# State reads of the sample group with 32 query columns as weights, updates by 32 rows, and waits for the tile that is needed

## The chip, the cores and the metric

The kernel runs on one NeuronCore of a Trainium2 chip. It is one launch, and the time is what the device takes for it, in microseconds. The figure quoted is the median of repeated runs. A profile is taken of one further execution, and its durations are those of that execution alone.

The engines that matter here are the tensor engine (PE; its weight loads are listed apart as PEld), the vector engine (DVE), the scalar engine (ACT), GpSimd (POOL) and the sync engine (SP), which issues all DMAs. Each works off its own list of instructions in order and waits on semaphores for the others.

## The reference

Two layers of a decoder trunk are applied to 320 tokens: one prompt of 256, and 8 sample sequences of 8 tokens each. In each layer three mixers of 4 heads carry a state of 128x128 per sequence and head (A: mLSTM, B: retention, C: a gated linear recurrence). For mixer B, in short:

```python
s = jnp.einsum('bthd,bshd->bhts', qc, kc) * dec
o = jnp.einsum('bhts,bshv->bthv', s, vc) + jnp.einsum('bthk,bhkv->bthv', qc, S) * inter
S_new = chunk_dec * S + jnp.einsum('hs,bshk,bshv->bhkv', to_end, kc, vc)
```

So each head reads its state (`qc` times `S`) and updates it (`k` times `v`, weighted). A and C do the same with other weights, and A also divides by a normaliser. A fourth branch (D) is a short convolution. Each layer then has gates, projections, two layer norms and a feed-forward part of width 4096. All weights and data are float32.

## The kernel before, in words

Activations stand with features on the 128 partitions and the 320 tokens along the free dimension (`T`, columns 256 to 319 are the samples). The big products go through 181 weight slots a layer (`SLOTS`). A slot is one 128x1024 block of weights. It is brought by DMA into a ring of three, split into a high part (`whi`, by ACT or DVE) and a low part (`wlo`, by POOL), and used in three products of 320 columns for each of its 8 blocks (lines 1179 to 1181) into one of three banks `gps`. A finished output is a tile; ACT or DVE takes it out of its bank and counts that in `tile_free`.

The mixers run as stages between the slots. `schedule_of_layer` writes the order once: a stage stands behind a slot when its inputs are there and some slots have passed since the last one (`COST`). Each stage is a list of phases by engine (`PHASES`), and each phase names the phases for which it waits; every finished phase is counted in `mix_done`. The banks `xp0` to `xp4` belong to the stages.

Two stages of each of the 24 heads (12 a layer) are changed:

- `num` reads. PE transposes the keys into `xp0` (`turn`, line 1290), adds up scores times values in `xp3` (`weigh`, lines 1301 to 1303), and adds the state reads (line 1364): for each of the 8 sequences a matmul that loads the 128x128 state `s0` as weights and streams 8 columns of `qw`, the weighted queries. ACT then copies the keys to `kt` (line 660) and the result on. DVE makes `vm` (line 1006), the sample values once per sequence, masked, 64x1024.
- `fin` updates. PE forms the prompt's new state (line 1375) and the samples' 8 updates (line 1383), two matmuls with 64 rows and 512 columns. DVE adds them into `s0` (line 1027), and SP sends it out and loads the state of the head after the next into the same buffer.

In mixer A a stage `a_score` and in B `b_rope` and `b_score` (line 1295 is the scores' first matmul, line 984 the last operation of `b_rope` on DVE) go ahead of `num`; `a_sq` (A) and `b_mean` (B) come between `num` and `fin`. In A `vm` is made in `a_sq`.

An f32 matmul is one instruction and shows as two records in the trace. Its form, as 128*128, is the part of the array it uses: rows times columns.

Beside the phases' own waits stands `settled`. Ahead of every stage's matmuls, and of a stage whose first phase is on ACT or DVE, the engine waits until all tiles up to the previous slot have left their banks:

```python
n = layer * NTILE + tile - tiles_in(i) - crossed(i)
for e in ("act", "dve"):
    if freed(e, n):
        eng.wait_ge(tile_free[e], freed(e, n))
```

Line numbers here and in the rows are those of this kernel; the changed one has its own, in the rows on the change.

## Time and profile before

| | |
|---|---|
| median of 3 runs | 1700.25 us (1698.64 to 1701.16) |
| the profiled execution | 1694.1 us, of which the span from first to last instruction is 1692.3 |
| PE busy | 1599.3 us, 95% of the span |
| PEld busy | 1520.7 us, 90% |
| DVE busy | 925.0 us, 55% |
| ACT busy | 648.0 us, 38% |
| POOL busy | 899.0 us, 53% |
| granted clock of PE, mean | 0.965 of full speed |
| L1364, state reads | 384 records |
| L1383, updates | 96 records |

A matmul's duration in the profile includes the time it spends in the pipeline, so durations of consecutive ones overlap. What a stretch costs on PE is read from the distance between starts. A line of the timeline merges equal neighbours: its first number is the first start, the second the time from there to the last end, and x is the count. The idle time ahead of a line, with what released it, stands in brackets.

### The profile page before, as it was taken

The numbers are of one execution on the slowest core, as the hardware profiler recorded it, in microseconds if no ns is written. First come the engines' busy times: TensorE is split into PE (matmuls) and PEld (weight loads), VectorE is DVE, ScalarE is ACT, GpSimd is POOL, SyncE is SP. The second block draws the span as 40 slices with busy tenths as digits, with TensorE's granted clock in tenths as the row PEclk, the third lists the DMA queues.
The fourth block names the chain that finished last, engine by engine and source line by source line (L and its number), as shares of the span: only waits on it lengthen the run. The fifth ranks groups of instructions, "written<-read, shape, count | busy, mean of one in ns | idle before, by whom it ended". The sixth has DMA issues, their size and how long they took to land.

```text
span 1692.3 us, 25612 instructions
## 1 busy us (share of the span) xinstructions
PE 1599.3 (95%) x10258; PEld 1520.7 (90%) x10258; DVE 925.0 (55%) x1717; ACT 648.0 (38%) x1166; POOL 899.0 (53%) x390
## 2 busy tenths in 40 slices
PE   7899999999999879999898999999999998799997
PEld 7899989998899869999797998889989997799996
DVE  4864774246766864422547657643457669544124
ACT  5434343333434343333354344333334343334333
POOL 6455453434445556666755554433444555566664
PEclk9999998999999989999999999989989999899998
DMA  7333443333444424444433334433334443344442
GB/s 271 111 116 108 165 155 113 114 114 127 129 160 142 125 87 150 150 150 150 128 121 110 104 115 163 141 116 111 114 115 153 127 138 115 97 150 150 150 150 82
DMA packets 66254, 223.57 MB, mean 132 GB/s; under 512 B 8024, under 2 KB 12632, under 8 KB 66136
## 3 DMA queue, kind: packets, MB, share of 16 engines
q1 hardware_dynamic: 66136, 221.93, 41.3%
q8 instruction: 82, 1.34, 0.3%
q14 instruction: 36, 0.29, 0.1%
HBM read 206.33 MB, written 15.58 MB: 131 GB/s over the span
## 4 chain that ended last, share of the span: by engine, by line
PE 80%; DVE 14%; ACT 2%; issue 2%; DMA 0%; SPq 0%; DVEq 0%; ACTq 0%
PE gps L1179 22%; PE gps L1180 21%; PE gps L1181 21%; PE xp L1383 3%; PE xp L1364 3%; DVE mix L918 1%; PE xp L1324 1%; PE xp L1384 1%; PE xp L1301 1%; DVE rs L1074 1%; PE xp L1303 1%; DVE whi L778 1%; PE xp L1375 1%; DVE mix L806 1%; DVE mix L1109 1%
## 5 line engine op out<-in xcount | busy, mean ns | idle before, releaser
L550 POOL TENSOR_TENSOR wlo<-raw,whi 128x1024 fp32r<-128x1024 f32 x362 | 878.0, 2427 | 765.4 <-ACT whi L571 463.3
L1179 PE MATMUL gps<-xh,whi 128*128 128x320 f32 x2000 | 649.7, 325 | 43.9 <-DVE xl L1119 22.4
L1180 PE MATMUL gps<-xl,whi 128*128 128x320 f32 x2000 | 631.5, 316 | 0.0
L1181 PE MATMUL gps<-xh,wlo 128*128 128x320 f32 x2000 | 631.1, 316 | 0.0
L571 ACT ACTIVATE whi<-raw 128x1024 fp32r<-128x1024 f32 x258 | 273.3, 1059 | 516.0 <-PE gps L1181 456.2
L1179 PEld LDWEIGHTS gps<-xh,whi 128*128 128x128 f32 x2000 | 389.0, 194 | 52.9 <-issue 31.7
L1180 PEld LDWEIGHTS gps<-xl,whi 128*128 128x128 f32 x2000 | 388.9, 194 | 3.2 <-issue 0.4
L1181 PEld LDWEIGHTS gps<-xh,wlo 128*128 128x128 f32 x2000 | 387.8, 194 | 0.0
L1179 PE MATMUL gps<-ah,whi 128*128 128x320 f32 x640 | 200.5, 313 | 0.5
L1180 PE MATMUL gps<-al,whi 128*128 128x320 f32 x640 | 199.1, 311 | 0.0
L1181 PE MATMUL gps<-ah,wlo 128*128 128x320 f32 x640 | 199.1, 311 | 0.0
L1179 PEld LDWEIGHTS gps<-ah,whi 128*128 128x128 f32 x640 | 121.3, 190 | 1.8 <-DVE al L841 0.8
L778 DVE CAST whi<-raw 128x1024 fp32r<-128x1024 f32 x104 | 76.4, 734 | 84.5 <-PE gps L1181 57.3
L1180 PEld LDWEIGHTS gps<-al,whi 128*128 128x128 f32 x640 | 121.4, 190 | 0.3
L1181 PEld LDWEIGHTS gps<-ah,wlo 128*128 128x128 f32 x640 | 121.4, 190 | 0.0
L824 DVE TENSOR_TENSOR mix<-mix,gps 128x320 f32<-128x320 f32 x32 | 15.6, 488 | 162.4 <-PE gps L1181 162.0
L819 DVE TENSOR_TENSOR gps<-gps,tt 128x320 f32<-128x320 f32 x64 | 32.0, 500 | 123.7 <-ACT tt L590 123.7
L597 ACT ACTIVATE tt<-gps,prm 128x320 f32<-128x320 f32 x64 | 33.8, 529 | 139.6 <-PE gps L1181 139.6
L1179 PE MATMUL gps<-yh,whi 128*128 128x320 f32 x256 | 80.9, 316 | 3.4 <-DVE al L841 2.1
L1180 PE MATMUL gps<-yl,whi 128*128 128x320 f32 x256 | 79.0, 309 | 0.0
L1181 PE MATMUL gps<-yh,wlo 128*128 128x320 f32 x256 | 79.0, 309 | 0.0
L1019 DVE COPY pst<-xp 128x128 f32<-128x128 f32 x24 | 7.0, 292 | 90.0 <-PE xp L1384 90.0
(271 smaller groups left out, 1925.2 us busy)
## 6 DMA issues: line engine op xcount, KB each, us to landing
raw<-in_w SPq DMA_DIRECT2D x362, 512.0 KB, 3.5
s<-in_st SPq DMA_DIRECT2D x24, 512.0 KB, 4.5
out_ss<-s SPq DMA_DIRECT2D x24, 512.0 KB, 2.7
con<-in_cst SPq DMA_DIRECT2D x4, 526.0 KB, 5.4
out_sp<-pst SPq DMA_DIRECT2D x24, 64.0 KB, 2.6
mix<-in_x SPq DMA_DIRECT2D x4, 320.0 KB, 5.0
out_y<-mix SPq DMA_DIRECT2D x8, 160.0 KB, 1.9
ee<-in_cst SPq DMA_DIRECT2D x1, 224.0 KB, 3.8
```

The source lines that it names most:

```text
L550: nc.gpsimd.tensor_tensor(wlo[:, c % RING, :, :], raw[:, c % RING, :, :], whi[:, c % RING, :, :].bitcast(F32), ALU.subtract).then_inc(lo_d ...
L571: nc.scalar.activation(whi[:, c % RING, :, :], raw[:, c % RING, :, :], ACT.Copy).then_inc(hi_done["act"], 1)
L597: link(nc.scalar.activation(t, ps, ACT.Abs, bias=prm[:, layer, PBG + j:PBG + j + 1]))
L778: V.tensor_copy(whi[:, c % RING, :, :], raw[:, c % RING, :, :]).then_inc(hi_done["dve"], 1)
L806: link(V.tensor_tensor(mix[:, a, :], xh[:, a, :].bitcast(F32), xl[:, a, :].bitcast(F32), ALU.add))
L819: link(V.tensor_tensor(ps, ps, t, ALU.mult))
L918: done(V.tensor_tensor(z, b, b[:, :, 0:1].to_broadcast([P, T // 4, 4]), ALU.subtract))
L1179: M(out, hi, xhi, start=start, stop=False)
L1180: M(out, hi, xlo, start=False, stop=False)
L1181: return M(out, lo, xhi, start=False, stop=stop)
L1364: last = M(xp[3][:, SEQ + b * DS:SEQ + (b + 1) * DS], s0[:, j % 2, b, :], qw[:, h, s], start=False, stop=b == NB - 1, skip_group_check=True)
L1383: M(xp[1 + i][:, :], kt[0:NS, 2, :], vm[:, 4 * i:4 * i + 4, :], start=True, stop=True)
```

## The change

The state reads swap sides. The weights are now 32 columns of `qw`, from the first query of a sequence on, and the state streams past them as 128 moving columns. The result is 32x128; only its first 8 rows belong to the sequence, the others are not used. Four such matmuls go to the four column strips of the array (`tile_position` (0, 32 i)) and to the four groups of 32 partitions of `xp4`, two rounds for 8 sequences. `qw` is 24 columns wider for it, zeroed once. ACT copies the 128x256 result to `seen`, and two matmuls with `seen` as weights and 32 chosen columns of the identity add it, turned, to `xp3`. The reads stand ahead of the transposes now.

The updates use row strips. `vm` holds 4 sequences side by side instead of 8 (64x512): the upper 32 rows belong to sequences 0 to 3, the lower to 4 to 7. Four matmuls of 32 rows and 256 columns replace two of 64 and 512, and alternate between the row strips and between banks `xp1` and `xp2`. The masks are folded to 4 columns (`same`, `fade` once, `own` once a head of A).

`settled` waits for the last tile that the stage uses (`last_tile_of`), and only in the stage's first phase. `num` has five phases instead of three, in C and B for instance:

```diff
-    "numC": (("pe", ("fin", -1, 1)), ("act", (0, ("fin", -1, 3))), ("dve", 0)),
-    "numA": (("pe", (("a_score", 0, 3), ("fin", -1, 2))), ("act", 0), ("dve", 1)),
-    "a_sq": (("act", ("num", 0, 2)), ("dve", ("num", 0, 0))),
-    "numB": (("pe", (("b_score", 0, 1), ("fin", -1, 2))), ("act", (0, ("fin", -1, 3))), ("dve", 0)),
-    "b_mean": (("pe", ("num", 0, 1)), ("dve", 0), ("act", 1)),
-
-    "finC": (("pe", (("num", 0, 1), ("num", 0, 2))), ("dve", 0), ("act", (0, ("fin", -1, 3))), ("dve", 2)),
...
+    "numC": (("pe", ("fin", -1, 2)), ("act", 0), ("pe", ("fin", -1, 1)), ("act", (2, ("fin", -1, 3))), ("dve", 2)),
...
+def last_tile_of(stage, n, h):
+
+    if n == "D":
+        return LTILES.index(("in", "bD", h) if stage == "conv" else ("br", "A", KD - 1))
+    name = {"c_log": ("in", "fC", 2 * h + 1), "c_first": ("in", "qC", h), "a_gate": ("in", "ifA", 0),
+            "a_score": ("in", "kA", h), "b_rope": ("in", "kB", h), "num": ("vt", "v" + n, h),
+            "fin": ("in", {"C": "gC", "A": "oA", "B": "gB"}[n], h)}.get(stage)
+    return None if name is None else LTILES.index(name)
...
-        def settled(eng, layer, tile, i):
-
-
-            n = layer * NTILE + tile - tiles_in(i) - crossed(i)
+        def settled(eng, layer, stage, n, h):
+
+
+            last = last_tile_of(stage, n, h)
+            if last is None:
+                return
+            n = layer * NTILE + last + 1
...
                elif stage == "num" and k == 1:
+                    done(nc.scalar.activation(seen[:, :, :], xp[4][:, 0:2 * P].rearrange("p (r c) -> p r c", r=2), ACT.Copy))
+                elif stage == "num":
...
-                        ends, mask = (ee[:, 255:256], ee[:, 383:384]), ee[0:NS, 384 + DS - 1:SP4:DS]
+                        ends, mask = (ee[:, 255:256], ee[:, 383:384]), own[:, :]
+                        half = 384 + NQ * DS
+                        link(V.tensor_tensor(own[:, :], ee[0:NS, 384 + DS - 1:half:DS], ee[0:NS, half + DS - 1:SP4:DS],
+                                             ALU.add))
...
-                    done(V.tensor_tensor(vm[:, :, :], v_of(n, h, 2).unsqueeze(1).to_broadcast([NS, NB, P]),
-                                         mask.unsqueeze(2).to_broadcast([NS, NB, P]), ALU.mult))
+                    done(V.tensor_tensor(vm[:, :, :], v_of(n, h, 2).unsqueeze(1).to_broadcast([NS, NQ, P]),
+                                         mask.unsqueeze(2).to_broadcast([NS, NQ, P]), ALU.mult))
...
+            def read_states(j, h):
+
+                for r in range(2):
+                    for i in range(4):
+                        b = 4 * r + i
+                        q = qw[:, h, b * DS:b * DS + 32]
+                        last = M(xp[4][32 * i:32 * (i + 1), r * P:(r + 1) * P], q, s0[:, j % 2, b, :], start=True, stop=True,
+                                 tile_position=(0, 32 * i), skip_group_check=True)
+                return last
+
+            def add_states
...
+                pick = ident.rearrange("p (i t) -> p i t", t=32)[:, :, 0:DS]
+                for r in range(2):
+                    out = xp[3][:, SEQ + 32 * r:SEQ + 32 * (r + 1)].rearrange("p (i t) -> p i t", t=DS)
+                    last = M(out, seen[:, r, :], pick, start=False, stop=r == 1, skip_group_check=True)
+                return last
...
+                elif stage == "num" and k == 0:
+                    j = layer * HEADS_PER_LAYER + state_of(n, h)
+                    pe.wait_ge(s_in[j % 2], 16 * (j // 2 + 1))
+                    done(read_states(j, h))
                 elif stage == "num":
-                    j = layer * HEADS_PER_LAYER + state_of(n, h)
                     turn(xp[0], z12[:, 1, h, :] if n == "C" else k_of(n, h))
-                    pe.wait_ge(s_in[j % 2], 16 * (j // 2 + 1))
                     weigh(xp[3], lambda i: v_of(n, h, i), h)
-                    for b in range(NB):
-                        s = slice(b * DS, (b + 1) * DS)
-                        last = M(xp[3][:, SEQ + b * DS:SEQ + (b + 1) * DS], s0[:, j % 2, b, :], qw[:, h, s],
-                                 start=False, stop=b == NB - 1, skip_group_check=True)
+
+                    follow(pe, layer, [("act", rows[1][2])])
+                    last = add_states()
...
-                    for i in range(2):
-                        M(xp[1 + i][:, :], kt[0:NS, 2, :], vm[:, 4 * i:4 * i + 4, :], start=True, stop=True)
+                    for j in range(0, NQ, 2):
+                        for i in range(2):
+
+                            rows = slice(32 * i, 32 * (i + 1))
+                            M(xp[1 + i][:, j * P:(j + 2) * P], kt[rows, 2, :], vm[rows, j:j + 2, :], start=True,
+                              stop=True, tile_position=(32 * i, 0), skip_group_check=True)
...
-                        settled(pe, layer, tile, slot_i)
-                        phase(*item[1:], layer, lambda ins: ins.then_inc(mix_done["pe"], 1))
+                        if k == 0:
+                            settled(pe, layer, *item[1:])
+                        phase(*item[1:], k, layer, rows, lambda ins: ins.then_inc(mix_done["pe"], 1))
```

On PE, the second head of mixer C in the first layer, before: stage `num`. The names after the arrow are the operands, `con` is the constants, among them the identity, `mix` the keys of C, `pt` the scores.

```order
L1290 MATMUL xp<-con,mix 128x128 [waits tile_free_dve,tile_free_act,mix_done_dve]
L1290 MATMUL xp<-con,mix 128x128
L1290 MATMUL xp<-con,mix 64x128
L1301 MATMUL xp<-pt,vc 128x256 [waits s_in0]
L1302 MATMUL xp<-pt,vc 128x128
L1303 MATMUL xp<-pt,vc 128x64
L1364 MATMUL xp<-qw,s 128x8 x8
```

Stage `fin` of the same head, a weight slot later, with the slot's product ahead and behind:

```order
L1181 MATMUL gps<-xh,wlo 128x320
L1375 MATMUL xp<-vc,kt 128x128 [waits tile_free_act,tile_free_dve,mix_done_dve,mix_done_act]
L1375 MATMUL xp<-vc,kt 128x128
L1383 MATMUL xp<-vm,kt 128x512 x2
L1384 MATMUL xp<-sq,ones 128x320
L1179 MATMUL gps<-xh,whi 128x320 [waits tile_free_act,lo_done]
```

`num` now:

```order
L1339 MATMUL xp<-s,qw 32x128 [waits s_in0,tile_free_act,mix_done_act]
L1339 MATMUL xp<-s,qw 32x128 x7
L1318 MATMUL xp<-con,mix 128x128 [waits mix_done_dve]
L1318 MATMUL xp<-con,mix 128x128
L1318 MATMUL xp<-con,mix 64x128
L1329 MATMUL xp<-pt,vc 128x256
L1330 MATMUL xp<-pt,vc 128x128
L1331 MATMUL xp<-pt,vc 128x64
L1348 MATMUL xp<-con,seen 128x32 [waits mix_done_act]
L1348 MATMUL xp<-con,seen 128x32
```

And `fin` now:

```order
L1209 MATMUL gps<-xh,wlo 128x320
L1422 MATMUL xp<-vc,kt 128x128 [waits tile_free_act,tile_free_dve,mix_done_dve,mix_done_act]
L1422 MATMUL xp<-vc,kt 128x128
L1433 MATMUL xp<-vm,kt 128x256 x4
L1435 MATMUL xp<-sq,ones 128x320
L1207 MATMUL gps<-xh,whi 128x320 [waits tile_free_act,lo_done]
```

The reads have moved from behind the weighing to the head of the stage, the load of the state (`s_in0`) is waited for there, and two matmuls with a wait on ACT end it. The updates are four instead of two.

On PE, `b_score` of B's first head, before and now:

```order
L1181 MATMUL gps<-yh,wlo 128x320
L1295 MATMUL xp<-zc 128x256 [waits tile_free_dve,tile_free_act,mix_done_dve]
L1296 MATMUL xp<-zc 128x128
L1297 MATMUL xp<-zc 64x64
L1179 MATMUL gps<-yh,whi 128x320 [waits tile_free_dve,lo_done]
```

```order
L1209 MATMUL gps<-yh,wlo 128x320
L1323 MATMUL xp<-zc 128x256 [waits mix_done_dve]
L1324 MATMUL xp<-zc 128x128
L1325 MATMUL xp<-zc 64x64
L1207 MATMUL gps<-yh,whi 128x320 [waits tile_free_dve,lo_done]
```

The matmuls are the same; the waits on `tile_free` are gone.

On DVE, the last of a gate tile and stage `a_sq` of A's first head, before and now:

```order
L828 TENSOR_SCALAR gps<-gps,prm 128x320 [waits act_part]
L829 TENSOR_TENSOR tt<-gps,tt 128x320 [waits dve_chain]
L1005 TENSOR_SCALAR vw<-va,ee 128x128 [waits mix_done_pe]
L1005 TENSOR_SCALAR vw<-va,ee 128x128
L1006 TENSOR_TENSOR vm<-va,ee 64x1024
L832 TENSOR_TENSOR mix<-gps,zc 128x320 [waits slot_done,gate_ready,tile_free_dve] x2
```

```order
L850 TENSOR_SCALAR gps<-gps,prm 128x320 [waits act_part]
L851 TENSOR_TENSOR tt<-gps,tt 128x320 [waits dve_chain]
L1021 TENSOR_TENSOR own<-ee 64x4 [waits mix_done_pe]
L1030 TENSOR_SCALAR vw<-va,ee 128x128 [waits dve_chain]
L1030 TENSOR_SCALAR vw<-va,ee 128x128
L1031 TENSOR_TENSOR vm<-va,own 64x512
L854 TENSOR_TENSOR mix<-gps,zc 128x320 [waits slot_done,gate_ready,tile_free_dve] x2
```

One small sum and a wait for it are new, and `vm` is half as wide.

## Rows read from the trace of the kernel before

**Rows 1.** The page, parts 1 and 4: busy time by engine, the chain by engine.

```profile
PE 1599.3 (95%) x10258; PEld 1520.7 (90%) x10258; DVE 925.0 (55%) x1717; ACT 648.0 (38%) x1166; POOL 899.0 (53%) x390
...
PE 80%; DVE 14%; ACT 2%; issue 2%; DMA 0%; SPq 0%; DVEq 0%; ACTq 0%
```

**Rows 2.** The waits of PE: line, releaser, us in total, times, longest.

```profile
PE gps L1179 <- DVE xl L1119: 22.4, 3, 7.9
```

**Rows 3.** Timeline of PE, `num` of C: start, us, engine, line, what.

```profile
158.55 0.31 PE L1181 MATMUL gps<-xh,wlo 128*128 128x320 f32 x1
158.70 0.49 PE L1290 MATMUL xp<-con,mix 128*128 128x128 f32 x3
159.02 0.60 PE L1301 MATMUL xp<-pt,vc 128*128 128x256 f32 x2
...
160.13 1.95 PE L1364 MATMUL xp<-qw,s 128*128 128x8 f32 x16
161.94 0.39 PE L1179 MATMUL gps<-xh,whi 128*128 128x320 f32 x1
```

**Rows 4.** Timelines of PE and of its weight loads, `fin` of the same head.

```profile
165.54 0.60 PE L1375 MATMUL xp<-vc,kt 128*128 128x128 f32 x4
166.08 1.98 PE L1383 MATMUL xp<-vm,kt 64*128 64x512 f32 x4
167.99 0.81 PE L1384 MATMUL xp<-sq,ones 128*128 128x320 f32 x2
...
168.78 0.30 PE L1180 MATMUL gps<-xl,whi 128*128 128x320 f32 x1
...
166.62 0.19 PEld L1383 LDWEIGHTS xp<-vm,kt 64*128 64x128 f32 x1 [0.24 <-issue]
167.04 0.19 PEld L1383 LDWEIGHTS xp<-vm,kt 64*128 64x128 f32 x1 [0.24 <-issue]
```

**Rows 5.** L1317, records of form 128*64: window, us, busy (x) of PE, PEld.

```profile
88.24:88.85 0.61, 0.61 (x9) 0.54 (x8) 1.00 0.00 0
```

**Rows 6.** Timelines of ACT and PE, `num` of the first head of A, second layer.

```profile
1098.68 0.49 PE L1290 MATMUL xp<-con,za 128*128 128x128 f32 x3
...
1100.32 0.46 ACT L622 ACTIVATE zc<-tt 128x320 f32<-128x320 f32 x1
1104.38 0.39 ACT L660 ACTIVATE kt<-xp 128x256 f32<-128x256 f32 x1 [3.61 <-PE xp L1368]
```

**Rows 7.** Timeline of PE: five of the seven waits ahead of `fin` and `b_score`.

```profile
279.19 0.68 PE L1375 MATMUL xp<-vw,kt 128*128 128x128 f32 x4 [1.28 <-issue]
...
387.38 0.68 PE L1375 MATMUL xp<-vw,kt 128*128 128x128 f32 x4 [2.00 <-DVE zc L792]
...
470.89 0.67 PE L1295 MATMUL xp<-zc 128*128 128x256 f32 x2 [0.72 <-DVE tt L829]
...
1227.94 0.35 PE L1375 MATMUL xp<-vw,kt 128*128 128x128 f32 x1 [1.73 <-DVE zc L792]
...
1250.74 0.45 PE L1295 MATMUL xp<-zc 128*128 128x256 f32 x1 [0.51 <-DVE tt L829]
```

**Rows 8.** Timeline of DVE ahead of three of them.

```profile
277.88 1.21 DVE L1006 TENSOR_TENSOR vm<-va,ee 64x1024 f32<-64x1024 f32 x1
...
385.63 1.21 DVE L1006 TENSOR_TENSOR vm<-va,ee 64x1024 f32<-64x1024 f32 x1
386.76 0.47 DVE L792 TENSOR_TENSOR zc<-gps,tt 128x320 f32<-128x320 f32 x1
...
468.92 0.23 DVE L984 TENSOR_TENSOR qw<-zc,con 128x64 f32<-128x64 f32 x1
...
470.25 0.49 DVE L829 TENSOR_TENSOR tt<-gps,tt 128x320 f32<-128x320 f32 x1
```

**Rows 9.** DMA queue and line L521: the state of the third head.

```profile
174.48 0.34 SPq L521 DMA_DIRECT2D s<-in_st  x1
...
DMA to landing us min/median/max: 3.5/4.6/5.8
```

More of the change, by code:

```diff
@@ L367, in trunk @@
         ee = sb("ee", [P, SP4])
-        vm = sb("vm", [NS, NB, P])
+        vm = sb("vm", [NS, NQ, P])
+        own = sb("own", [NS, NQ])
+        same = sb("same", [NS, NQ])
+        fade = sb("fade", [NS, H, NQ])
         kt = sb("kt", [P, 3, P])
@@ L375, in trunk @@
         tt = sb("tt", [P, BANKS, T])
-        qw = sb("qw", [P, H, NS])
+        qw = sb("qw", [P, H, NS + 32 - DS])
         qn = sb("qn", [P, NS])
+        seen = sb("seen", [P, 2, P])
         dec = sb("dec", [P, H, NB])
@@ L743, in _ @@
                         if k == 0:
-                            settled(act, layer, tile, slot_i)
+                            settled(act, layer, *item[1:])
                         phase(*item[1:], k, layer, lambda ins: ins.then_inc(mix_done["act"], 1))
@@ L939, in phase @@
                     V.tensor_tensor(z12[:, 1, :, :], z12[:, 1, :, :], zc[:, 1, :, :], ALU.mult)
[L940 removed]
+                    done(V.tensor_tensor(qw[:, :, 0:NS], qw[:, :, 0:NS], zc[:, 0, :, SEQ:T], ALU.mult))
                 elif stage == "a_gate" and k == 1:
@@ L1152, in _ @@
                             dve.wait_ge(small_in, 64)
+                            each = c_("vmask", NS).rearrange("p (h b) -> p h b", h=H)
+                            V.tensor_tensor(same[:, :], c_("seqmask", NS)[:, 0:NQ], c_("seqmask", NS)[:, NQ:NB], ALU.add)
+                            V.tensor_tensor(fade[:, :, :], each[:, :, 0:NQ], each[:, :, NQ:NB], ALU.add)
                             V.tensor_copy(negb[:, :], ee[:, :]).then_inc(setup_dve, 1)
@@ L1169, in _ @@
                         if k == 0:
-                            settled(dve, layer, tile, slot_i)
+                            settled(dve, layer, *item[1:])
                         phase(*item[1:], k, layer, lambda ins: ins.then_inc(mix_done["dve"], 1))
```

26 lines of the change are left out of this document (17 added, 9 removed).

## The prediction

> **What bounds the kernel now.** I read the chain of waits first. It lies on the tensor engine for 80% of the span, and that engine is busy for 95% of it [rows 1]. Then the tensor engine's own waits: they are few and short, the largest being 22.4 us at the layer norms [rows 2]. So in the part of the program that the change touches, what the tensor engine issues is what counts. A microsecond taken from its stream there is a microsecond of the run, and one added likewise. The vector and scalar engines matter only where the tensor engine waits for them.
>
> Third, the timeline of the tensor engine in one head's two stages. An f32 matmul shows as two records. Two records with 256 moving columns take 0.44 us (159.02 to 159.46), 0.22 each, so 128 columns cost 0.107 a record and 512 cost 0.43. The state reads are 8 matmuls, 16 records with only 8 moving columns, and yet take 1.81 us (160.13 to 161.94): 0.113 each, the time of loading 128 weight columns [rows 3].
>
> The update products take 1.91 us (166.08 to 167.99) for four records of 512 columns. Two of its weight loads stand 0.42 apart (166.62 and 167.04), so the streaming is four times 0.427, 1.71, and 0.2 is something else. From L1375's start to L1180's after the stage are 3.24 us. Streaming explains 0.43 (L1375) + 1.71 + 0.53 (two records of 320) + 0.15 (one weight-slot record, 158.55 to 158.70 [rows 3]) = 2.82. The other 0.42 is two changes of the shape in which the array is used, 128*128 to 64*128 and back: 0.21 for each change [rows 4].
>
> **The change, part by part**
>
> **Updates (24 heads).** Two matmuls of 64 rows by 512 columns become four of 32 rows by 256, alternating between rows 0 to 31 and 32 to 63 of the array. The streamed columns stay 1024, so one behind the other they cost the old 1.71 us. Fully side by side they cost half, 0.85. Which it is, no row shows: nothing in this program uses two parts of the array at once. What the rows show is that each matmul is two records, and the second needs the same part of the array as the first. It can start only when the first has streamed. So I expect that the next matmul, in the other rows, starts beside the *second* record. A matmul then costs one record (0.213) plus the least distance between two starts. Eight records of 64 columns with their changes of shape passed in 0.61 us, 0.076 each [rows 5], so that distance is between 0 and 0.076, and I take 0.04. Four matmuls: 4 x 0.253 + the tail (0.213 - 0.04) = 1.19 us, against 1.71. That is -0.52 a head, **-12.5 us**. The changes of shape around it stay two, except in the eight heads of mixer A, where a 64-row matmul (L1380) stands just ahead: one more at 0.21 each, **+1.7**.
>
> **Reads (24 heads).** The 16 records of 0.113 go. In their place come 8 matmuls whose weights are 32 columns and whose moving side is 128, 16 records of 0.107, put into the four column strips in turn. End to end that is 1.71 us, four abreast 0.43. By the same argument as above (second record beside the next matmul's first): 8 x (0.107 + 0.04) + (0.107 - 0.04) = 1.24. They stand ahead of the transposes now, between two full-array stretches, so they bring two changes of shape that were not there: 2 x 0.21 = 0.42. The transposing products at the end are two matmuls, four records with 128 weight columns loaded: 4 x 0.113 = 0.45. Sum 0.42 + 1.24 + 0.45 - 1.81 = +0.30 a head, **+7.2 us**. So this part, which looks like the main one, I expect to lose. Its ends: -0.51 a head four abreast (-12.2), +0.77 end to end (+18.5).
>
> **The new hand-over.** Between the reads and the transposing products the scalar engine copies 128x256 out of the bank. This is the added wait. What is queued behind it on the tensor engine is the rest of the head and all weight slots. The same copy by size is L660's 0.39 us, and I allow 0.2 for the two hand-overs. The scalar engine is the later one: in the worst of the 24 places its queue is busy until 2.10 us after the slot's end (1098.68 to 1100.78) [rows 6]. Copy done: 2.10 + 0.39 + 0.2 = 2.69 at worst. The tensor engine needs it after 0.21 + 1.24 + 0.21 + 1.43 (transposes and weighing, 158.70 to 160.13 [rows 3]) = 3.09. So it is hidden, by 0.4 us at the tightest, and I cost it at nothing. If the reads ran four abreast the cover would be gone there: 0.4 us in four heads of 24 (the first two of mixer A in each layer), 1.7 us in all. The copy itself (24 x 0.39 = 9 us of a 38% busy engine) hides there too.
>
> **Exact waits.** Until now each stage waited until all tiles up to the previous slot were out of their banks. Now it waits for its own. The places where the tensor engine really stood there are seven: 1.28, 2.00, 0.72, 1.28, 1.73, 0.51 and 0.72, 8.2 us together ([rows 7]; the second 1.28 and the second 0.72 read as the first). I take them one by one. The three at L1295 end with a gate tile's L829 (470.25 + 0.49), although what the scores need, L984, was done at 469.15 [rows 8]: all of it goes, 1.95. The two of 1.28 end with the vector engine's vm (277.88 + 1.21 = 279.09), which is needed: the wait stays, but vm is halved to 64x512. That takes off 0.6 less about 0.2 for the added small sum "own" and the link behind it: 0.4 each. The two of 2.00 and 1.73 end with an eviction (L792) behind vm (until 386.84): next comes vm, itself 0.4 earlier, so 387.23 - 386.4 = 0.8, twice. Together 1.95 + 0.8 + 1.7 = **-4.5 us** (ends 0 and -8.2). What is late next is vm in both.
>
> The earlier read of the state needs its load 1.4 us sooner. The load for the third head is issued at 174.48 and lands at most 5.8 us later [rows 9]; the reads come after 192. It costs nothing. The halved vm frees about 14 us of a vector engine that is 55% busy, worth nothing beyond the waits named. Two tiny sums at the start are nothing either.
>
> **Sum.** -12.5 + 1.7 + 7.2 - 4.5 = -8.1 us. The profiled run took 1694.1 us (span 1692.3 and 1.8 around it), so 1686.0. The median of the runs is 1700.25, 6.2 above the profiled one. The same difference there gives **1692.2**.
>
> **The rivals**
>
> *Four (and two) abreast.* The two records of a matmul don't hold up its neighbours: reads -12.2, updates (0.85 - 1.71) x 24 + 1.7 = -18.9, waits -4.5, sum -35.6, time 1665. For it: strips hold separate weights. Against it: the pairs of records in one strip, in issue order.
> By the Trainium skill ("TensorE: Matmul & The Clock Gate", Part 3: Packing small matmuls) matmuls in different strips start about 4 ns apart, three column strips (it calls them tiles) gave 2.38 times and four row strips 3.07 times the pace. No run here shows that yet. By its ratios I estimate 1.71 / 3.17 = 0.54 for the reads and 1.71 / 1.54 = 1.11 for the updates, which would make the time about 1674. It measured them with matmuls of one record, and these have two, which is why I hold to the other sum.
>
> *Nothing overlaps (slower).* The strips run one after the other, as all records in the trace do. The place is the 24 read stages: 0.42 + 1.71 + 0.45 - 1.81 = +0.77 each, +18.5; updates 0 + 1.7; waits -4.5. Sum +15.7, time 1716. It decides from the point where a read matmul costs more than about 0.19 us instead of 0.147: the reads then eat what updates and waits give. For it: every record of this trace, and the four shape changes of a head; against it: nothing measured here.
>
> *Only rows overlap.* The update pairs run side by side, the column strips don't: +18.5 - 10.8 - 4.5 = +3.2, time 1703.5, at the edge of no change. For it: the column strips share the rows by which the moving data comes in, the row strips don't.
>
> *The copy isn't hidden* would add at most 0.4 us in each of four heads, too little to be a case of its own.
>
> **How the numbers follow.** Forecast 0.50, abreast 0.17, nothing overlaps 0.15, only rows 0.13, something unseen 0.05. The forecast's own range is 1684 to 1700, from the ends of the starting distance (0 to 0.076: reads and updates +-0.04 x 12 starts x 24 = +-11, less at the low end as tails shorten) and of the waits. The range for the time is **1666 to 1712**. It leaves out most of the abreast case's lower half and the upper half of "nothing overlaps", under 2 in 10 together. A difference within 0.2% (3.4 us) can't be told from none here. Faster by more: 0.85 of the forecast, all of abreast, a little else, 0.62. Within: 0.14. Slower: nothing overlaps, half of "only rows" and some of the unseen, 0.24.
>
> **What would show it.** In the profile after: the read group (now 32-column weights, x16) should take about 1.2 us and not 0.5 or 1.7, with about 0.2 ahead of and behind it. The update group (now x8 records of 256 columns) should take about 1.4 us from its start to L1384's successor, against 1.91. The wait at the scores should be gone, the ones at the first update product of A be about 0.9 and 1.2. No wait on the copy "seen".  The prediction is wrong if the read stage is where time is saved, or if a wait on the scalar engine appears ahead of the transposing products.

## The result, and the profile after

The kernel with all three parts of the change takes **1633.98 us** (median of 4 runs, 1631.16 to 1635.6). The kernel before took 1699.45 beside it (4 runs, 1698.21 to 1701.16). The ratio is **0.9612, 95% interval 0.9596 to 0.9629**. The forecast was 1692.2 with a range of 1666 to 1712. The direction was right, but the gain is eight times as large, and the time lies below the whole range.

The page of the profile after, parts 1 and 4, answers to [rows 1]:

```profile
PE 1547.6 (95%) x10450; PEld 1483.6 (91%) x10450; DVE 927.1 (57%) x1727; ACT 653.4 (40%) x1190; POOL 900.8 (55%) x391
...
PE 84%; DVE 11%; ACT 2%; issue 2%; DMA 1%; SPq 0%; DVEq 0%; ACTq 0%
```

The tensor engine is still the bound, at the same share of a shorter span. Its busy time fell by 51.7 us. The view by core (span, mean granted clock), before and after:

```profile
core 0: 1692.3 us, clock 0.965
```

```profile
core 0: 1632.8 us, clock 0.975
```

The clock moved as well, and I come back to that. First the stages. The timeline of the tensor engine after, in `num` of the same head as [rows 3] (start, us from the first start to the last end, engine, line, operands, form, count):

```profile
156.18 0.31 PE L1209 MATMUL gps<-xh,wlo 128*128 128x320 f32 x1
156.42 0.65 PE L1339 MATMUL xp<-s,qw 128*32 128x128 f32 x16
157.00 0.55 PE L1318 MATMUL xp<-con,mix 128*128 128x128 f32 x3
...
158.49 0.63 PE L1348 MATMUL xp<-con,seen 128*128 128x32 f32 x4
158.96 0.39 PE L1207 MATMUL gps<-xh,whi 128*128 128x320 f32 x1
```

The 16 records of the reads pass in **0.58 us** (156.42 to 157.00). Sixteen records of 0.107 one after the other would be 1.71, so four are under way at any time: 0.43, and 0.15 for the change of shape behind them. By their single starts they begin in four waves of four, at 156.42, 156.56, 156.67 and 156.78. The stage took 3.24 us before (158.70 to 161.94) and takes 2.54 now. A further 0.09 stands ahead of it (156.18 to 156.42 is 0.24, where a slot record takes 0.15). The transposes behind the reads take 0.38 (157.00 to 157.38), where they took 0.32 [rows 3], and the turning products cost 0.47 (158.49 to 158.96).

Stage `fin` of the same head, where [rows 4] stood:

```profile
162.41 0.31 PE L1209 MATMUL gps<-xh,wlo 128*128 128x320 f32 x1
162.56 0.61 PE L1422 MATMUL xp<-vc,kt 128*128 128x128 f32 x4
163.09 1.13 PE L1433 MATMUL xp<-vm,kt 32*128 32x256 f32 x8
164.16 0.81 PE L1435 MATMUL xp<-sq,ones 128*128 128x320 f32 x2
164.56 0.55 PE L1207 MATMUL gps<-xh,whi 128*128 128x320 f32 x1
```

The update group takes 1.07 us (163.09 to 164.16) where it took 1.91. That is 0.85 for two abreast and 0.2 for the change of shape. From L1422 to the slot's first record are 2.00 us, where L1375 to the slot were 2.85 (165.54 to 168.39).

Next, the waits of the tensor engine within the mixer stages (us in all, times, longest). Before, beside the line of [rows 2]:

```profile
PE xp L1375 <- DVE zc L792: 3.7, 2, 2.0
PE xp L1317 <- ACT bd L611: 3.0, 2, 2.3
PE xp L1375 <- issue: 2.9, 4, 1.3
PE xp L1333 <- ACT af L650: 2.7, 2, 1.3
...
PE xp L1295 <- DVE tt L829: 1.9, 3, 0.7
PE xp L1324 <- DVE ud L846: 1.7, 4, 0.4
```

After:

```profile
PE xp L1422 <- issue: 5.1, 6, 1.3
PE xp L1379 <- DVE af L968: 2.5, 2, 1.3
...
PE xp L1348 <- ACT seen L679: 0.7, 4, 0.2
```

15.9 us have become 8.3, **-7.6**. (In another execution of this kernel, after_again below, they are 9.8: a wait of 1.5 us at L1363, for the stage's own input, is there in one layer and not in this profile. Differences of a microsecond or two in these sums are no effect of an edit.) The waits at the scores (L1295) are gone. So are two groups ahead of mixer C's chain of levels (L1317, L1324), 4.7 us, of which the forecast did not speak. The two longest waits ahead of the updates are now 1.28 and 1.29 us, the two of 1.28 now 0.99. Short waits on the copy `seen` are new.

**Where 59.5 us of span went.** Reads (0.09 - 0.70) x 24 = -14.6. Updates -0.85 in the 16 heads of C and B and -0.76 in the 8 of A, measured at full clock, -19.7. Waits -7.6. That is 41.9. The other **17.6 us** are spread over weight slots and stages of mixer A whose matmuls are the same in both kernels, and there the granted clock differs. It has two levels here, 2.4 GHz and 1.2. A mean clock of 0.965 over 1692.3 us means 2 x 0.035 x 1692.3 = 118 us at the lower one; after it are 2 x 0.025 x 1632.8 = 82 (each +-1.7, for the clock is given to three places). A microsecond at half clock costs up to half a microsecond (less where the engine would have waited anyway), so this is worth up to 18 us. What it did cost can be summed from the starts in the trace: for each record in such a stretch, the distance to the next start, less the median distance of the same two kinds of record at the full clock (distances over 1 us, which are waits, left out). That gives 44.0 us lost before and 29.1 after. **14.9** of the 17.6 are the clock by this sum, and 2.7 stay without a place.

What such a stretch looks like, in the first head of A in the second layer before, by windows (start:end and length; busy us and records of PE, PEld, DVE, ACT and POOL; then the granted clock, the DMA share and GB/s):

```profile
1098.70:1102.00 3.30, 3.30 (x27) 3.06 (x25) 1.75 (x3) 1.83 (x4) 2.28 (x1) 1.00 0.49 159
1102.00:1109.00 7.00, 7.00 (x27) 6.57 (x27) 3.13 (x3) 0.86 (x3) 0.07 (x1) 0.53 0.24 75
```

The first window is `num` with its 16 records of 8 moving columns, at the full 2.4 GHz. The second follows on it at 0.53, with the engine busy throughout. In the profile after, the same place:

```profile
1065.00:1069.30 4.30, 4.12 (x39) 3.32 (x38) 1.75 (x3) 2.10 (x5) 2.35 (x1) 1.00 0.39 122
1069.30:1076.00 6.70, 6.70 (x48) 6.70 (x48) 4.78 (x6) 2.70 (x7) 1.72 (x1) 1.00 0.27 78
```

48 records in 6.7 us, against 27 in 7.0. Over the whole trace of before, 9 of the 24 groups of reads (7 of them in mixer A) are followed by a stretch at 1.2 GHz that begins 2.1 to 3.8 us after the group's first record. These nine hold 44 of the 118 us. After, none of the 24 groups is followed so. What a slot record costs at the lower level is seen in the second layer's first `num` of C, before:

```profile
997.85 1.95 PE L1364 MATMUL xp<-qw,s 128*128 128x8 f32 x16
...
1000.32 0.47 PE L1179 MATMUL gps<-xh,whi 128*128 128x320 f32 x1
1000.59 0.47 PE L1180 MATMUL gps<-xl,whi 128*128 128x320 f32 x1
```

0.27 from start to start instead of 0.15, right behind the reads.

### The profile page after: what moved, and what is told of

It is laid out like the page before. It is cut to its first block, busy times and chain, and to the rows that moved or that the text cites. A ratio compares the mean times of both kernels' runs of the same rounds, so it can differ in the third digit from the quotient of the medians.

```text
span 1632.8 us, 25994 instructions
## 1 busy us (share of the span) xinstructions
PE 1547.6 (95%) x10450; PEld 1483.6 (91%) x10450; DVE 927.1 (57%) x1727; ACT 653.4 (40%) x1190; POOL 900.8 (55%) x391
## 4 chain that ended last, share of the span: by engine, by line
PE 84%; DVE 11%; ACT 2%; issue 2%; DMA 1%; SPq 0%; DVEq 0%; ACTq 0%
PE gps L1207 24%; PE gps L1208 23%; PE gps L1209 23%; PE xp L1433 2%; PE xp L1370 1%; PE xp L1435 1%; DVE mix L940 1%; PE xp L1348 1%; DVE rs L1099 1%; DMA raw<-in_w 1%; PE xp L1422 1%; DVE mix L828 1%; PE xp L1329 1%; PE xp L1339 1%; DVE mix L1134 1%
## 5 line engine op out<-in xcount | busy, mean ns | idle before, releaser
L1207 PEld LDWEIGHTS gps<-xh,whi 128*128 128x128 f32 x2000 | 384.1, 192 | 51.7 <-issue 29.6
L1208 PEld LDWEIGHTS gps<-xl,whi 128*128 128x128 f32 x2000 | 384.2, 192 | 3.2 <-issue 0.4
L1209 PEld LDWEIGHTS gps<-xh,wlo 128*128 128x128 f32 x2000 | 383.3, 192 | 0.0
L846 DVE TENSOR_TENSOR mix<-mix,gps 128x320 f32<-128x320 f32 x32 | 15.6, 488 | 162.0 <-PE gps L1209 161.6
L1207 PEld LDWEIGHTS gps<-yh,whi 128*128 128x128 f32 x256 | 48.6, 190 | 6.2 <-DVE al L863 3.1
```

Source lines behind the costliest of these rows:

```text
L1207: M(out, hi, xhi, start=start, stop=False)
L1208: M(out, hi, xlo, start=False, stop=False)
L1209: return M(out, lo, xhi, start=False, stop=stop)
```

## The experiments

Theories at the start: the strips stream fully abreast (against the forecast's order of starts), the new form of the reads and the order of the strips decide how much, and the clock carries the rest (against: it is waits or slots that shifted). The experiments ran in three groups on three chips, apart from the pair above. The kernel before ran beside each of them: 1693.0 us with updates_only, reads_only, waits_only and wide_reads, 1693.4 with updates_wide, one_strip, strip_runs and after_wide, 1693.1 with after_again, after_old_waits and after_fold. The kernel after took 1633.45 there, ratio 0.9645. A difference in us below is against the kernel before of the same group; where kernels of two groups are compared, the three medians of before show that the chips differ by less than half a microsecond. The stages' sums are over each kernel's own profile, against the profile of before. Time at the lower clock is 2 x (1 - clock) x span, and what was lost there is the sum over the starts, as above.

| kernel | median us | ratio, 95% | clock | us at the lower clock | us lost there | reads' stages | updates' stages | weight slots |
|---|---|---|---|---|---|---|---|---|
| before | 1693.0 to 1693.4 | 1 | 0.965 | 118 | 44.0 | | | |
| updates_only | 1678.81 | 0.9911 (0.9889 to 0.9933) | 0.957 | 144 | 52.3 | -2.2 | -23.9 | +11.1 |
| reads_only | 1667.04 | 0.9842 (0.9817 to 0.9867) | 0.973 | 90 | 30.3 | -19.0 | -0.2 | -10.2 |
| waits_only | 1685.32 | 0.9947 (0.9928 to 0.9966) | 0.966 | 114 | 41.3 | -0.5 | 0.0 | -7.9 |
| wide_reads | 1678.69 | 0.9916 (0.9889 to 0.9943) | 0.974 | 87 | 27.2 | -3.3 | +1.4 | -14.2 |
| updates_wide | 1654.57 | 0.9779 (0.9756 to 0.9801) | 0.972 | 93 | 28.6 | -3.3 | -21.9 | -13.2 |
| one_strip | 1663.91 | 0.9828 (0.9799 to 0.9857) | 0.976 | 80 | 25.1 | +10.7 | -22.2 | -20.3 |
| strip_runs | 1633.51 | 0.9654 (0.9628 to 0.9680) | 0.980 | 65 | 22.4 | -18.8 | -22.9 | -21.9 |
| after_again | 1633.45 | 0.9645 (0.9626 to 0.9663) | 0.977 | 75 | 26.6 | -19.3 | -22.4 | -19.6 |
| after_old_waits | 1647.49 | 0.9733 (0.9710 to 0.9757) | 0.971 | 95 | 32.9 | -18.5 | -22.0 | -8.4 |
| after_wide | 1634.50 | 0.9653 (0.9630 to 0.9675) | 0.976 | 78 | 26.8 | -19.1 | -20.9 | -18.9 |
| after_fold | 1627.63 | 0.9610 (0.9587 to 0.9633) | 0.982 | 58 | 17.1 | -19.2 | -27.3 | -21.6 |

The stages' columns hold waits within a stage and its share of the lower clock. The column of the weight slots holds what they lost to the lower clock and also the waits ahead of stages, so waits_only's -7.9 is mostly waits. The clock and the stages are those of one profiled execution each, and of before there is only the one of 1694.1 us. The clock is given for the other executions too, and its mean over them is steadier: 0.963 for before beside updates_only, which has 0.959 (125 and 138 us at the lower clock, 13 more and not 26). A sum of a row is good to a few microseconds, the ratios are not touched by it.

### The three parts, each alone

**updates_only**: the kernel before with the row strips and the halved `vm`, its reads and waits as they were.

```diff
-                    for i in range(2):
-                        M(xp[1 + i][:, :], kt[0:NS, 2, :], vm[:, 4 * i:4 * i + 4, :], start=True, stop=True)
+                    for j in range(0, NQ, 2):
+                        for i in range(2):
+                            rows = slice(32 * i, 32 * (i + 1))
+                            M(xp[1 + i][:, j * P:(j + 2) * P], kt[rows, 2, :], vm[rows, j:j + 2, :], ...,
+                              tile_position=(32 * i, 0))
```

> The kernel before with the 32-row updates alone. Overlap theory (records in different row strips stream fully side by side): the update group of a head takes 1.07 us instead of 1.91, fin stages together about 20 us shorter, so about 1680. Clock theory adds: the half-clock stretches behind num and a_score of mixer A stay, so the weight slots gain at most 4 us; 1674 to 1680. The rival that the updates bring all the gain would give 1640.

Measured: -14.2 us. The update group takes 1.06 us in its timeline (167.38 to 168.44), as in the kernel after: the updates' 19.7 us stand, and its `fin` stages are 23.9 shorter. But the slots, with the same matmuls, became 11.1 us longer, and more time lies at the lower clock: 8.3 us more are lost there. 15 of the 24 groups of reads are followed by such a stretch, where it was 9 before. The stages won more than the kernel did.

**reads_only**: the kernel after with the old updates and the old waits.

```diff
-                    for j in range(0, NQ, 2):
-                        for i in range(2):
...
+                    for i in range(2):
+                        M(xp[1 + i][:, :], kt[0:NS, 2, :], vm[:, 4 * i:4 * i + 4, :], start=True, stop=True)
...
+            n = layer * NTILE + tile - tiles_in(i) - crossed(i)
```

> The kernel before with the state reads of the changed kernel alone (swapped sides, four strips, copy, transposing products), old updates and old waits. Overlap theory: num stages 19 us shorter. Clock theory: most half-clock stretches of mixer A go as well, so the weight slots gain 10 to 18 us: 1663 to 1670 in all. Without the clock theory only the 19 us: 1680.

Measured: -26.0 us, where the forecast's term was +7.2. Reads and turning products are worth 14.6 by their rows. The other 11.4 go with 28 us less at the lower clock, where 13.7 us less are lost. `fin` is unchanged.

**waits_only**: the kernel before with `settled` of the kernel after.

```diff
-            n = layer * NTILE + tile - tiles_in(i) - crossed(i)
+            last = last_tile_of(stage, n, h)
+            if last is None:
+                return
+            n = layer * NTILE + last + 1
...
-                        settled(pe, layer, tile, slot_i)
+                        if k == 0:
+                            settled(pe, layer, *item[1:])
```

> The kernel before with the exact waits alone. The three waits at the scores go (1.95 us), the two behind an eviction shrink by up to 0.4 each, the rest stay because vm keeps its width: 2 to 3 us less, about 1697. If the waits were behind the gain in the weight slots, these would lose about 18 us: 1681.

Measured: 1685.32, some 8 us less. The expectation was too low, since it did not know of the waits ahead of the levels. In this kernel's waits L1317's counterpart waits once, 1.5 us, for its own input, and no longer for a tile's eviction; L1324's is not among them. In all 9.7 us are left of 15.9, so 6.2 are waits. 2.7 us less are lost at the lower clock, which is about the rest.

### Is it the clock?

**wide_reads**: the kernel before, and its state reads stream 64 columns instead of 8. This is more work for the array, and the results are not the reference's.

```diff
-                        s = slice(b * DS, (b + 1) * DS)
-                        last = M(xp[3][:, SEQ + b * DS:SEQ + (b + 1) * DS], s0[:, j % 2, b, :], qw[:, h, s],
+                        last = M(xp[3][:, SEQ:T], s0[:, j % 2, b, :], qw[:, h, :],
```

> The kernel before with 64 moving columns instead of 8 in each state read (every state is streamed against all 64 queries and summed, so the samples' outputs are not the reference's). The record stays bound by its weight load (0.113 us; 64 columns stream in 0.053), so num keeps its length. Clock theory: with more streaming in the same time the half-clock stretches behind num are fewer and the weight slots run 10 to 18 us shorter, 1682 to 1690. Rival (the clock has to do with the waits or the vector engine, not with how much the tensor engine streams): no change, 1700.

Measured: -14.2 us (0.9916). The timeline of its reads:

```profile
160.55 2.00 PE L1363 MATMUL xp<-qw,s 128*128 128x64 f32 x16
162.36 0.39 PE L1179 MATMUL gps<-xh,whi 128*128 128x320 f32 x1
```

1.81 us from the group's start to the next, to the hundredth what [rows 3] has for 8 columns: the weight loads set the pace. `num` has the same length as before in C and B (3.24 a head). What changed is the view by core:

```profile
core 0: 1676.0 us, clock 0.974
```

So 31 us fewer lie at the lower clock, 16.8 us less are lost there, and the slots are 14.2 us shorter, without one matmul less. The same place in mixer A as in the windows above, here:

```profile
1092.00:1095.30 3.30, 3.30 (x27) 3.06 (x26) 1.74 (x3) 1.82 (x4) 2.30 (x1) 1.00 0.50 159
1095.30:1102.30 7.00, 7.00 (x48) 6.76 (x48) 4.03 (x5) 2.67 (x7) 0.71 (x2) 1.00 0.23 75
```

The first window has the same 27 records and is as busy as before, and the second stays at the full clock. This is the clearest evidence that few moving columns cost time *behind* them. It explains what reads_only gained beyond its rows.

All profiles together say the same. In the three kernels whose reads stream 8 columns (before, updates_only, waits_only), 9, 15 and 7 of the 24 groups of reads are followed by a stretch at 1.2 GHz, which begins 1.9 to 3.8 us after the group's first record. In the ten whose reads stream 64 or 128, none of the 24 is, and one_strip is among them, whose 16 records stand one after the other as before. So the stretches go with what the reads stream, and not with how long the group lasts.

**updates_wide**: updates_only and wide_reads together (same two edits).

> The 32-row updates alone, with the state reads streaming 64 columns instead of 8 (outputs of the samples not the reference's). Alone the updates gave 14 us, though the stages got 25 shorter; the weight slots gave 11 back. Clock theory: that was half-clock time, and with more streaming in the reads it goes, so the two add up to more than 14 + 14: 1654 to 1658. If the give-back has another cause the parts add up at best: 1665 or more.

Measured: 1654.57, 24.2 below updates_only; the slots' +11.1 became -13.2, and 23.7 us less are lost at the lower clock. Against wide_reads the updates are now worth 24.1 us, where against the kernel before they were worth 14.2. The give-back of updates_only was the clock.

### Do the strips run abreast, and does the order matter?

**one_strip**: the kernel after with all eight reads in the first column strip and the first 32 partitions. It leaves the state reads of most sequences out of the result. The bank is zeroed once at the start.

```diff
+                            V.memset(xp[4][:, 0:2 * P], 0.0)
...
-                        last = M(xp[4][32 * i:32 * (i + 1), r * P:(r + 1) * P], q, s0[:, j % 2, b, :], ...,
-                                 tile_position=(0, 32 * i), skip_group_check=True)
+                        last = M(xp[4][0:32, r * P:(r + 1) * P], q, s0[:, j % 2, b, :], ...,
+                                 tile_position=(0, 0), skip_group_check=True)
```

> The changed kernel with all 8 read matmuls of a head in the same column strip (so seven of eight results are overwritten and the samples' outputs are not the reference's). Overlap theory: 16 records one after the other, 1.71 us instead of 0.43, so a num stage is 1.28 us longer, 31 us in all, about 1665; the clock has no part, since the records still stream 128 columns each. Rival (the gain of the reads is the clock's alone): about 1634 as before.

Measured: 1663.91, 30.5 above after_again. Its timeline:

```profile
157.87 1.93 PE L1340 MATMUL xp<-s,qw 128*32 128x128 f32 x16
159.74 0.55 PE L1319 MATMUL xp<-con,mix 128*128 128x128 f32 x3
```

1.87 us instead of 0.58, 1.29 x 24 = 31. The four strips are the whole difference, and the clock took no part in it (0.976 and 0.977; 25.1 and 26.6 us lost).

**strip_runs**: the kernel after with the matmuls of one strip in a row, in reads and updates. If starts follow the order of issue, a strip's second record holds up the others.

```diff
-                for r in range(2):
-                    for i in range(4):
+                for i in range(4):
+                    for r in range(2):
...
-                    for j in range(0, NQ, 2):
-                        for i in range(2):
+                    for i in range(2):
+                        for j in range(0, NQ, 2):
```

> The changed kernel with the matmuls in another order: both of a column strip in a row (reads), both of a row strip in a row (updates). If a later matmul waits for the ones issued before it to start (the prediction's rule), records start no earlier than their strip allows: reads about 13 x 0.107 = 1.4 us instead of 0.43, updates 7 x 0.213 = 1.5 instead of 0.85, together 1.6 us a head, up to 39 us: 1673. If the array takes up records of other strips out of order, nothing changes: 1634.

Measured: 1633.51 against 1633.45 of after_again. Its read and update groups:

```profile
157.14 0.67 PE L1339 MATMUL xp<-s,qw 128*32 128x128 f32 x16
157.74 0.55 PE L1318 MATMUL xp<-con,mix 128*128 128x128 f32 x3
...
163.84 1.14 PE L1433 MATMUL xp<-vm,kt 32*128 32x256 f32 x8
164.90 0.81 PE L1435 MATMUL xp<-sq,ones 128*128 128x320 f32 x2
```

0.60 and 1.06, against 0.58 and 1.07. By starts in the order of issue the reads would be strip behind strip: each strip has four records, the next one could begin only with the fourth, and the group would take 13 x 0.107 = 1.39. It does not. A record that waits for its strip holds up nothing in another strip, and the forecast's rule falls. (The trace doesn't name the strip of a record; this rests on the order of issue, on the group's length and on its first four starts, which lie within 0.04 us here too.)

The Trainium skill ("TensorE: Matmul & The Clock Gate", Part 3: Packing small matmuls) has matmuls in strict order of start and end. For these f32 pairs the run shows otherwise for the starts, since 0.60 is less than half of 1.39; the ends are not read here.

### What are the exact waits worth in the kernel after?

**after_old_waits**: the kernel after with `settled` of the kernel before (the edit of waits_only backwards).

> The changed kernel with the old waits on all tiles. The waits that come back: at the scores 2 us, at mixer C's levels 4.6 us, at the evictions ahead of A's fin about 1 us: 7 us more than the changed kernel, 1641. My prediction's count (scores and fin alone) would give 4.5.

Measured: 1647.49, 14.0 above after_again. The waits, in its own lines:

```profile
PE xp L1419 <- DVE zc L811: 3.5, 2, 1.7
PE xp L1360 <- ACT bd L628: 3.0, 2, 2.3
...
PE xp L1320 <- DVE tt L848: 2.1, 2, 1.0
PE xp L1367 <- DVE ud L865: 1.7, 4, 0.4
```

With the smaller ones 16.4 us in all. after_again has 9.8, so with 6.6 us more idle time the kernel is 14 us slower, twice what was expected. The other half goes with 20 us more at the lower clock, where 6.3 us more are lost. Which short wait brings which stretch was not isolated.

### A better kernel

**after_wide**: in mixer A's `fin` the normaliser's products stream one column each (L1425). Widened to 64, to try whether wide_reads' gain can be had there too.

```diff
-                            M(xp[0][:, P:P + 1], kt[:, i, :], ee[:, (255, 383)[i]:(256, 384)[i]], ...)
+                            M(xp[0][:, 192:256], kt[:, i, :], ee[:, (192, 320)[i]:(256, 384)[i]], ...)
```

> The changed kernel with 64 instead of 1 moving columns in the two normaliser products of mixer A's fin (L1425; the wanted column is the last, the result is the reference's). Those records are bound by their weight load, so the stage keeps its length. Clock theory: the half-clock stretches behind A's fin (three of the six that are left in the mixers) become fewer, 1.7 us each: 2 to 5 us less. Rival: they come from the waits ahead of fin, no change.

Measured: 1634.50, no gain. The clock is 0.976 (after_again 0.977), and A's `fin` is 1.5 us longer in all. Widening these four records a head brought nothing.

**after_fold**: the normaliser's products go altogether. Their column becomes the 129th of the value products, and the samples' product goes into two row strips.

```diff
+                        V.tensor_copy(vw[:, :, P:P + 1], ee[:, 255:384:128].unsqueeze(2))
...
-                        M(xp[0][:, 0:P], kt[:, i, :], v, start=i == 0, stop=False, skip_group_check=True)
+                        M(xp[0][:, 0:w_], kt[:, i, :], v, start=i == 0, stop=False, skip_group_check=True)
...
-                            M(xp[0][:, P:P + 1], kt[:, i, :], ee[:, (255, 383)[i]:(256, 384)[i]], ...)
...
+                            rows = slice(32 * i, 32 * (i + 1))
+                            out = (xp[0][:, P + 1:P + 1 + NQ], xp[3][:, 0:NQ])[i]
+                            M(out, kt[rows, 2, :], own[rows, :], start=i == 1, stop=True, tile_position=(32 * i, 0))
```

> The changed kernel with mixer A's normaliser products folded: the prompt's weight column goes with the values as a 129th moving column (four records of one column go, 0.43 us), and the samples' part becomes two 32-row matmuls in the two row strips instead of one of 64 rows (one change of the array's shape less, 0.2 us). About 0.6 us for each of 8 fin stages, 5 us, less up to 1 us that the small extra copy adds to the four waits ahead of fin: 4 us less than the changed kernel. Rival: the clock's half-speed stretches shift by as much, no difference.

Measured: **1627.63**, 5.8 us below after_again (its runs from 1623.21 to 1630.95, those of after_again from 1631.94 to 1634.3; the intervals of the two ratios still touch). A's `fin` in the profile after, second layer's first head:

```profile
1081.07 0.68 PE L1422 MATMUL xp<-vw,kt 128*128 128x128 f32 x4 [0.99 <-issue]
1081.59 0.50 PE L1425 MATMUL xp<-ee,kt 128*128 128x1 f32 x4
1082.02 0.39 PE L1427 MATMUL xp<-ee,kt 64*128 64x8 f32 x2
1082.34 1.13 PE L1433 MATMUL xp<-vm,kt 32*128 32x256 f32 x8
1083.40 1.06 PE L1435 MATMUL xp<-sq,ones 128*128 128x320 f32 x2
```

And in after_fold:

```profile
1074.57 0.68 PE L1426 MATMUL xp<-vw,kt 128*128 128x129 f32 x4 [1.07 <-issue]
1075.18 0.39 PE L1431 MATMUL xp<-own,kt 32*128 32x4 f32 x4
1075.42 1.11 PE L1437 MATMUL xp<-vm,kt 32*128 32x256 f32 x8
1076.46 1.03 PE L1439 MATMUL xp<-sq,ones 128*128 128x320 f32 x2
```

From its first matmul to the last line 1.89 us instead of 2.33. That is 0.44 in each of 8 heads, 3.5 us. In its profile 17 us fewer lie at the lower clock (12 by the means over all executions) and 9.5 us less are lost there, but waits ate part of it: among others one of 1.5 us at the scores (L1326, for `qw`) is new. So only the 3.5 us are sure to be the edit's.

**after_again** is the kernel after, unchanged, beside these.

> The changed kernel once more, on the same chip as its variants: 1634 where before takes 1699, or the same ratio, 0.961 to 0.965.

Measured: 1633.45, on a chip where the kernel before takes 6 us less than beside the pair. The difference is in the kernel before alone. Its one profile (1694.1 us, clock 0.965) has the time and the clock of these chips: over the 27 executions of before beside the experiments the clock is 0.960 to 0.970, 0.964 in the mean. The clock of the four executions beside the pair is not on record, so whether it made them 6 us slower stays open. Among the 27, the span is about 0.27 us shorter for each microsecond less at the lower clock (correlation 0.83). That is the same kernel throughout, and it is of the same order as the 0.36 that the starts give (44.0 lost of 118).

## Why the prediction was wrong

**What bounds the kernel: right.** What was saved in the tensor engine's stream came off the span, and nothing on another engine took its place.

**Updates: right in direction, too small.** Forecast -0.52 a head and 1.19 for the streaming. Measured -0.85, and 0.85 for the streaming. The step that failed in the reads failed here too.

**Reads: the sign was wrong, and here lies the step that failed.** It is this one: "It can start only when the first has streamed. So I expect that the next matmul, in the other rows, starts beside the *second* record." The first sentence holds within a strip. The second does not follow: the next matmul begins beside the *first* record, 0.01 us after it. In one strip the 16 read records take 1.87, in four 0.58 (one_strip), in either order of the strips (strip_runs). So the reads stream in 0.43 us and not in 1.24, and the term of +7.2 is -14.6. The forecast took a limit within one strip for a limit of the whole array. The rival "four abreast" had the mechanism right, and I gave it 0.17. For the other order there was an argument and no row at all. Even that rival's 1665 is 31 us above the result: its sum of -35.6 lacks 6.3 us of shape changes and waits (below) and all of the clock, and its base was the median of before, 1700.25, where the profiled run took 1694.1.

The estimate by the Trainium skill's ratios ("TensorE: Matmul & The Clock Gate", Part 3: Packing small matmuls) was 1674. I set it aside because I took them to come from matmuls of one record. Here two records make no difference: the streaming takes 0.43 and 0.85, less than the 0.54 and 1.11 estimated.

**Shape changes: too dear.** Forecast 0.21 each wherever the form changes. In the updates that holds (0.2 for the pair's group, as before). But around the reads the first costs 0.09, and the second 0.15 and 0.06 more in the transposes behind it, 0.30 in place of 0.42. The extra one in mixer A, from 64 to 32 rows, costs about 0.1 (0.85 - 0.76). That is 24 x 0.12 + 8 x 0.1 = 3.7 us overrated. With the turning products at 0.47 instead of 0.45 it accounts for the reads: -12.2 was the forecast's sum for four abreast, -14.6 was measured.

**The hand-over: right within a microsecond.** It was to be hidden, and if the reads ran abreast to show in four heads, 1.7 us in all. They do run abreast, and the view of waits has it in four heads, the first two of mixer A in each layer, 0.7 us in all. By the distance from L1331's start to L1348's (0.36 where nothing is waited for) it costs 0.22 to 0.26 in these four and 0.08 to 0.15 in three heads of C, 1.3 us. One of the four, on PE and ACT:

```profile
1067.37 0.63 PE L1348 MATMUL xp<-con,seen 128*128 128x32 f32 x4 [0.18 <-ACT seen L679]
```

```profile
1066.60 0.45 ACT L642 ACTIVATE zc<-tt 128x320 f32<-128x320 f32 x1
1066.96 0.36 ACT L679 ACTIVATE seen<-xp 128x256 f32<-128x256 f32 x1
```

**Exact waits: nearly right where it looked (-3.7 of -4.5), but it did not look everywhere.** The three waits at the scores went (1.9). The two of 1.28 became 0.99 (forecast 0.9). The 2.00 became 1.28 (forecast 1.2) and the 1.73 became 1.29 (forecast 0.9). The list of seven, however, was made of waits ahead of `fin` and `b_score`, while `settled` stands ahead of every stage. The 4.7 us at L1317 and L1324 end with a tile's eviction too, by ACT L611 and DVE L846, and went with the others, but for a wait of up to 1.5 us for L1363's own input.

**The clock: no term at all.** The profile said 0.965, and the table ahead of the prediction lists it. I treated it as a constant, since the change left the slots alone. In truth 118 us of the run before lay at half clock, 44 of them in stretches right behind reads, and the change took 36 us of the 118 away. With 14.9 us by the starts (17.4 in after_again), this is the largest item that the forecast missed after the reads. That the clock follows the matmuls was shown by wide_reads, which changes nothing else.

By the forecast's own form the sum would have been -14.6 - 19.7 - 7.6 = -41.9, time 1652 on the profiled run.

**Open.** The three parts alone give 14.2 + 26.0 + 7.7 = 48 us, together 60. Most of the 12 between them is the clock: of what is lost at the lower clock, updates_only adds 8.3 us and reads_only and waits_only take off 13.7 and 2.7, 8.1 less in all, where after_again has 17.4 less. For the other 3 there is no run. By its stages and waits (14.1 us left of 15.9) updates_only should gain 21.5 and gains 14.2, so 7 went back, and the 8.3 cover it. Not known is why only 31 of the 72 groups with 8 columns (three kernels) were followed by a stretch, and what brings the stretches that remain after.

## What to carry to other kernels

If many small matmuls each load a full set of weights for a few moving columns, swap the sides so that the few columns are the weights, and put them into different strips. The streaming shrinks by the number of strips (here 1.71 to 0.43 us), in either order tried, also for f32; the changes of shape come on top. A granted clock below 1 in the profile is a term of the sum: turn it into microseconds at the lower level, look at what the tensor engine did ahead of each stretch, and ask for each edit whether it removes or adds such work. And when a rule for waiting is replaced, list every place where the old rule was the last to be met, from the view of waits, not only the stages that the rest of the change touches.

## What the runs showed of the hardware that was not expected

- Four column strips gave 1.87 / 0.58 = 3.2 times the pace, the change of shape included, and two row strips 1.91 / 1.07 = 1.8 times, with two records to a matmul.
- Streaming 64 columns instead of 8 behind the same weight loads costs nothing (1.81 us for 16 records either way) and made the kernel 14 us faster through the clock. By the Trainium skill ("TensorE: Matmul & The Clock Gate", Part 1: The HAM clock gate) the clock follows how busy the engine has been. The profile's busy share agrees with that only in part: PE was busy for 3.30 of 3.30 us ahead of a stretch at 0.53.
- With 6.6 us more of short waits after_old_waits is 14 us slower, and 20 us more lie at the lower clock.
- A microsecond at the lower clock cost 0.36 us in the profile before (44.0 of 118) and as much after (29.1 of 82), less than the half that the ratio of the clocks suggests.
